# Identity multiplies on TensorE in front of waits, in a two-block transformer kernel

## The reference, cut to what matters

```python
def layer(x, xc, ...):                       # first block, twice; xc is a context of 256 tokens
    h  = modulate(x, g_norm1, sh1, sc1)      # rms norm, gain and shift
    hc = modulate(xc, g_norm1, ...)
    proj, projc = h @ w_in, hc @ w_in[:, :n_in_c]
    k, v, q = mixer_kv(...), mixer_q(...)    # low-rank latents, norms per head, rotary
    o_mla, o_gqa = blocked_attend(...), blocked_attend(...)
    o_four = fourier_mix(...)
    x = x + gt1 * merge_branches(o_mla, o_gqa, o_four, gate_cols, lp)
    x = x + gt2 * conv_ffn(modulate(x, g_norm2, sh2, sc2), lp)
    # the same for xc in layer 0 alone

def second_block(x, ...):
    for layer in range(2):                   # mixer ab: dilated attention and a gated scan
        y = _mixer_ab(x, ...) if layer == 0 else _mixer_c(x, ...)
        x = _layer_norm(DEEPNORM_ALPHA * x + y, ln_gain[layer], ln_bias[layer])
    return x
```

## Time and profile before

| | |
|---|---|
| three runs | 1990.22, 1991.87 and 1993.07 us; median 1991.87 |
| profiled execution, first to last instruction (span) | 1988.9 us; no time of its own is given beside it, the three runs lie 1.3, 3.0 and 4.2 us above |
| TensorE products, busy | 1877.4 us (94%), 12063 records |
| TensorE weight loads, busy | 1571.9 us (79%) |
| VectorE, ScalarE, GpSimd busy | 1162.5, 933.1 and 198.5 us |
| mean granted clock of TensorE | 0.983 |
| DMA | 265.36 MB, mean 133 GB/s |

### The profile page before, as it was taken

One profiled execution on the slowest core, in us unless ns is written; L12 is line 12 of the kernel. 1 busy time (PEld: TensorE's weight loads), 2 busy tenths in 40 slices (PEclk: granted clock), 3 DMA queues, 4 the chain that ended last, 5 costly groups with the idle time before them and its releaser, 6 DMA issues.

```text
span 1988.9 us, 31268 instructions
## 1 busy us (share of the span) xinstructions
PE 1877.4 (94%) x12063; PEld 1571.9 (79%) x12063; DVE 1162.5 (58%) x1802; ACT 933.1 (47%) x1427; POOL 198.5 (10%) x203
## 2 busy tenths in 40 slices
PE   5999999999998999999998889989999999899997
PEld 2875565788887888888784579989989888799996
DVE  3326566444346555523535456677744578789987
ACT  3327555323324333311436654455534656387782
POOL 4010001000011223210100000023301000100000
PEclk9999999999998999999998999989999999999999
DMA  9225668333332232232250036645557433444442
GB/s 310 91 80 169 197 221 273 97 95 95 90 110 81 89 102 94 96 116 95 85 170 6 1 88 177 191 143 181 178 190 217 158 118 104 150 151 146 146 137 101
DMA packets 262855, 265.36 MB, mean 133 GB/s; under 512 B 6342, under 2 KB 230960, under 8 KB 262752
## 3 DMA queue, kind: packets, MB, share of 16 engines
q1 hardware_dynamic: 257856, 249.32, 40.4%
q0 software_dynamic: 4448, 13.49, 2.2%
q10 hardware_dynamic: 448, 1.12, 0.2%
HBM read 262.81 MB, written 1.10 MB: 133 GB/s over the span
## 4 chain that ended last, share of the span: by engine, by line
PE 78%; DVE 12%; ACT 5%; DMA 2%; issue 2%; SPq 0%; DVEq 0%; ACTq 0%
PE bank L480 21%; PE bank L481 21%; PE bank L482 21%; PE bank L693 4%; DVE weights_fine L1839 2%; PE bank L710 2%; DMA region<-in_w_mod 2%; PE bank L538 2%; PE bank L474 2%; PE bank L527 2%; PE bank L700 1%; ACT weights_coarse L1137 1%; DVE region L2482 1%; DVE small L2164 1%; PE bank L950 0%
## 5 line engine op out<-in xcount | busy, mean ns | idle before, releaser
L1839 DVE TENSOR_TENSOR weights_fine<-region,weights_coarse 128x2048 fp32r<-128x2048 f32 (+2 forms) x181 | 417.7, 2308 | 346.8 <-ACT weights_coarse L1137 345.7
L1137 ACT CAST weights_coarse<-region 128x2048 fp32r<-128x2048 f32 (+3 forms) x185 | 355.0, 1919 | 333.0 <-PE bank L482 323.9
L480 PE MATMUL bank<-normed_coarse,weights_coarse 128*128 128x256 f32 (+1 forms) x1104 | 371.3, 336 | 9.2 <-DVE normed_fine L1977 4.3
L481 PE MATMUL bank<-normed_fine,weights_coarse 128*128 128x256 f32 (+1 forms) x1104 | 370.9, 336 | 0.0
L482 PE MATMUL bank<-normed_coarse,weights_fine 128*128 128x256 f32 (+1 forms) x1104 | 370.8, 336 | 0.0
L480 PEld LDWEIGHTS bank<-normed_coarse,weights_coarse 128*128 128x128 f32 x1104 | 212.4, 192 | 30.7 <-issue 10.1
L481 PEld LDWEIGHTS bank<-normed_fine,weights_coarse 128*128 128x128 f32 x1104 | 212.3, 192 | 20.5
L482 PEld LDWEIGHTS bank<-normed_coarse,weights_fine 128*128 128x128 f32 x1104 | 212.3, 192 | 20.4
L480 PE MATMUL bank<-x_turned_coarse,weights_coarse 128*128 128x256 f32 x616 | 177.8, 289 | 8.7 <-DVE weights_fine L1839 4.2
L481 PE MATMUL bank<-x_turned_fine,weights_coarse 128*128 128x256 f32 x616 | 175.5, 285 | 0.0
L482 PE MATMUL bank<-x_turned_coarse,weights_fine 128*128 128x256 f32 x616 | 175.5, 285 | 0.0
(11 more groups left out here) (295 smaller groups left out, 3574.4 us busy)
## 6 DMA issues: line engine op xcount, KB each, us to landing
region<-in_w_mod SPq DMA_DIRECT2D x48, 1024.0 KB, 5.3
region<-in_w_up SPq DMA_DIRECT2D x44, 1024.0 KB, 5.1
region<-in_w_in_c SPq DMA_DIRECT2D x30, 1024.0 KB, 5.2
region<-in_w_in_ab SPq DMA_DIRECT2D x20, 1024.0 KB, 5.3
region<-in_w_in SPq DMA_DIRECT2D x32, 512.0 KB, 4.7
region<-in_w_down SPq DMA_DIRECT2D x16, 1024.0 KB, 5.0
region<-in_w_in SPq DMA_DIRECT2D x14, 1024.0 KB, 5.0
region<-in_w_in SPq DMA_DIRECT2D x16, 384.0 KB, 3.5
```

The source lines that it names most:

```text
L480: nc.tensor.matmul(o, sc, mc, start=first, stop=False)
L481: nc.tensor.matmul(o, sc, mf, start=False, stop=False)
L1137: nc.scalar.copy(w_co[:, p, 0:size], raw_w[:, s, 0:size]).then_inc(coarse_ready, 1)
L1839: nc.vector.tensor_tensor(w_fi[:, p, 0:size], raw_w[:, s, 0:size], w_co[:, p, 0:size].bitcast(F32), ALU.subtract).then_inc(fine_ready, 1)
```

## The change

A helper `keep_busy(n)` is added to TensorE's stream. It multiplies the identity (`ident`, 128x128, float32) by itself n times into the first 128 columns of bank 7, each time as a new sum. It waits for nothing, signals nothing, and nobody reads the result. It is called in 16 places in the course of the program, 144 multiplies in all: before the first norm (9) and in it (4), at the last transposes of layer 0's second norm (11) and behind it (9), in layer 1's first norm (12), before the last head transposes of layer 1 (8), before both attentions (6 each), before layer 1's merge (9), before its second norm (10), in it (4) and behind it (18), and in the two `turn_x` (3 and 7; 22 and 6). No other engine's stream is changed.

```diff
--- before.py
+++ after.py
@@ -556,6 +556,11 @@
                     pe.wait_ge(bank_read[b], n)
                 transposes([first_rows[:, m * P:(m + 1) * P] for m in range(4 * pair, 4 * pair + 4)], parts_in=MOD_ROWS)
 
+            def keep_busy(n):
+
+                for _ in range(n):
+                    nc.tensor.matmul(pb[7][:, 0:P], ident[:, :], ident[:, :], start=True, stop=True)
+
             def xn_transposes(t):
                 seen_next(xn_ready)
                 for half in range(2):
@@ -577,9 +582,12 @@
             def norm(nt, project=False, started=0):
 
                 for t in range(nt):
+                    if t == nt - 1 and not project:
+                        keep_busy(11 if nt == 4 else 4)
                     if t >= started:
                         xn_transposes(t)
                     if project and t == 1:
+                        keep_busy(4 if started else 12)
                         w = split_weights(KD, COLS)
                     if project and t >= 1:
                         seen_next(h_ready)
@@ -656,6 +664,8 @@
                         following = products(*tiles[s + 1])
                     if l == 0:
                         mod_chunk()
+                    elif s + 1 == len(tiles):
+                        keep_busy(8)
                     mla_transposes(kind, t, raw[s % 2], copied)
                     gqa_transposes(kind, t)
 
@@ -868,29 +878,38 @@
             xn_transposes(0)
             first_product(7)
             first_transposes(3)
+            keep_busy(9)
 
             for l in range(DEPTH):
                 norm(4, project=True, started=int(l == 0))
                 project(l)
                 latents(l)
                 heads_prep(l)
+                keep_busy(6)
                 attend(l)
                 if l == 0:
                     mod_chunk(last=True)
                     reads = list(u.reads)
                 fourier(l, (lambda: gate_transposes(reads)) if l == 0 else None)
+                if l:
+                    keep_busy(9)
                 merge(l)
                 mix_out(l)
+                if l:
+                    keep_busy(10)
                 norm(items_of(l))
+                keep_busy(18 if l else 9)
                 ffn_up(l)
                 ffn_down(l)
 
 
-            def turn_x(updates_of):
+            def turn_x(updates_of, idle):
                 for t in range(2):
+                    keep_busy(idle[t])
                     for half in range(2):
                         pe.wait_ge(x_done, updates_of(t, half))
                         transposes([x_tok[:, t, k * P:(k + 1) * P] for k in range(4 * half, 4 * half + 4)])
+                keep_busy(idle[2])
                 evacuated()
 
             def features():
@@ -992,7 +1011,7 @@
                             w.append([v.rearrange("p (k n) -> p k n", k=WIDE_ROWS) for v in (last_co, last_fi)])
                         end(token_rows(accs[t][:, :], y2T, WIDE_ROWS * part, t, w[half], WIDE_ROWS, WIDE, False, True))
 
-            turn_x(lambda t, half: X_UPDATES - 1 + t)
+            turn_x(lambda t, half: X_UPDATES - 1 + t, (0, 3, 7))
             w = split_weights(KD, P)
             feature_product(w, KD, 0, xT, SEQ)
             for _ in range(4):
@@ -1043,7 +1062,7 @@
             seen_next(y_ready)
             out_last(rest)
 
-            turn_x(lambda t, half: X_UPDATES + 2 * t + half + 1)
+            turn_x(lambda t, half: X_UPDATES + 2 * t + half + 1, (0, 22, 6))
             for _ in range(3):
                 features()
             tokens()
```

## The result

The changed kernel took 1978.62 us (median; 1978.16 to 1979.29 in 4 runs) against 1991.9 (1990.22 to 1993.07). The ratio is 0.9925, 95% interval 0.9911 to 0.9938: faster by 0.75%, some 13.3 us where 16.9 were forecast, and inside the range of 1969 to 1984. The profiled execution has a span of 1976.8 us against 1988.9, 12.1 less.

The account below looks back on a forecast made before the run. TensorE, busy 94% of the span, was taken to bound the kernel, with nine stretches at half clock. Their gains of 17.7 us less 1 for new falls, off the 1991.9 median, gave 1975.2, said as 1975.0; range 1969 to 1984.

Parts of the forecast that it names:

- The price of a multiply: In the blocks: 0.223 us each at full clock, 0.43 at half; 144 multiplies add 32 us of TensorE work.
- The blocks fit: In the 16 places: blocks fill 80 to 95% of a hole and end before the awaited event at full clock.
- the block of 4 in the last norm: Before the transposes at 1301.13: 0.9 us in a 0.28 us hole delays them 0.6 us, but costs nothing.
- VectorE takes over: In the norms (44.6): VectorE's chain limits the gain to its idle 1.93 and 0.65 us before line 1959: 2.5 us.
- rival 2: All nine low stretches: every microsecond at half clock is worth half itself, 30.7 us of 61.5, giving 1961; chance 0.04.
- the term for falls that come anew: At two long holes left open (1052.95 and 1633.17): falls cost 1.5 us each, perhaps 3; counted as 1 us.
- The open hole before 1621: The unfilled 2.80 us hole before the products at 1633.17 in the old kernel; a fall would cost 1.5 us, perhaps 3.
- the first (some falls come anew): Any place: some falls stay or come anew, four stretches at 2 us each, gain 9, giving 1983; chance 0.14.
- The fourth: Behind the stretches: regained time is lost at once because weights and loads come no earlier, giving 1989; chance 0.06.
- The third: In the blocks: identity products don't hold the clock, run at 0.43 us each and overrun by 9.6, giving 2001.5; chance 0.06.

Follow-up runs that it names:

- the last of the kernels with more blocks: The changed kernel plus blocks of 10 in two open holes, single multiplies among the 32-row products, and blocks of 7 in four layer 0 holes: 1979.68 us.

## Why the prediction was right, and what it missed

The forecast was 1975.0 us and the chance 0.70 went to 1971 to 1979; 1978.62 lies at the upper end of that. The mechanism held, stretch by stretch. The distance in time between the same VectorE instruction in the two profiles, read before and behind each place (positive: the changed kernel is ahead), gives what each stretch brought:

| stretch before | distance, before it and behind it | measured | forecast |
|---|---|---|---|
| 44.6 | -1.78, 0.66 | 2.4 | 2.5 |
| 198.2 | 0.67, 2.34 | 1.7 | 1.8 |
| 604.4 | 2.88, 5.12 | 2.2 | 2.3 |
| 976.5 | 5.12, 7.40 | 2.3 | 2.4 |
| 1078.9 | 7.40, 10.67 | 3.3 | 2.6 |
| 1171.0 | 10.64, 12.13 | 1.5 | 1.5 |
| 1300.7 | 12.05, 13.62 | 1.6 | 1.8 |
| 1502.1 | 13.62, 14.80 | 1.2 | 1.3 |
| 1717.2 | 10.36, 12.14 | 1.8 | 1.5 |
| sum | | 17.9 | 17.7 |

**The price of a multiply** taken from the scan's products (0.223) held: 0.22 in the blocks. **The blocks fit**: the stalls left are 0 to 0.8 us (up to 0.6 were forecast), and the block of 4 in the last norm behaved as the steps said, the transposes come at once behind it (1289.54, no idle time) and VectorE's readers lose nothing by it. **VectorE takes over** in the norms: its idle time of 1.93 us is gone and the 0.65 is 0.24. That a low stretch is worth what the chain through it gives, and not half its length, was the step that separated 1975 from rival 2's 1961: 17.9 us came of 61.5.

What the prediction had too small is the term for falls that come anew, 1 us in the sum. By the same distances it measured 4.4. The open hole before 1621 cost 1.4 (11.77 to 10.36), just what the prediction had put on one such fall. The fall at 1529.0 cost 3.0 (14.80 to 11.77) and stood in no step: the prediction took idle time as the one cause of a fall, and the kernels with 32 rows showed that work on few rows does it too. The second profile of the changed kernel gives 1.5 and 3.0 us for the same two falls.

A second term, at nothing in the prediction, is the start of the program, where VectorE's distance goes to -1.78 before the first block. TensorE's timeline there, of the kernel before and then of the changed one:

```profile
35.81 1.04 PE L538 MATMUL bank<-region,sil_c 128*2 128x256 f32 x16 [1.68 <-DMA region<-in_w_mod]
36.78 1.44 PE L474 MATMUL bank<-ident,region 98*128 98x98 f32 x12
...
35.94 1.89 PE L538 MATMUL bank<-region,sil_c 128*2 128x256 f32 x16 [1.35 <-DMA region<-in_w_mod]
37.76 2.62 PE L474 MATMUL bank<-ident,region 98*128 98x98 f32 x12
```

The same sixteen passes and twelve transposes took nearly twice as long. TensorE still worked at its slow pace from the start, which the kernel before had left by 35.81; the table of stretches doesn't show this, as it gives 1.00 there. The change has no part in it, no block runs before 42.53: in the second profile of the changed kernel the same rows take 1.04 and 1.44 us, and its span is 1974.0. So 1.3 of the 1.8 us are this pace (the distance was -0.46 before), and it is an accident of the execution.

The account of the spans is then 17.9 for the stretches, less 4.4 for the new falls, less 1.8 for the start, and 0.5 more in the attention of layer 0, where waits for weight loads shrank: 12.2, against 12.1 measured. The medians differ by 13.3. The profiled run of the changed kernel took 1.8 us more than its span; with the same addition, an estimate, the profiled execution of the kernel before took 1990.7, 1.2 less than its median. So the forecast missed by the two terms above, 3.4 and 1.8 us, and was helped by small ones the other way, 1.2 of it in the base; that it came out no further off than 3.6 is in part luck. The first term is a real gap in the reasoning.

Of the rivals, the first (some falls come anew) is what took part of the gain, with two new stretches at 4.4 us together where it had four at 2 us each. The fourth has one instance, the wait for a load at 335 us in the last of the kernels with more blocks. The third is true of blocks with 32 rows and false of these. The second is refuted by 17.9 us against its 30.7.

Why the clock holds through one open hole in an execution and falls at it in another stays open. The kernel before held through 2.80 and 2.84 us and fell after 1.48; the changed kernel held through 2.84 and fell behind 2.80.

## What to carry to other kernels

Read the granted clock in short stretches, and price a stretch at half clock by the chain through it. Filling the waits in front of such stretches with idle multiplies pays when they end before the event, at a price taken from a like product of the same trace; beyond the hole they cost nearly their full length, and at half clock twice that. Let the filler use all 128 rows: 32 failed, and no number between was tried. The columns may be few, and float32 transposes do as well. Real products on few rows can bring the clock down by themselves.

## What the runs showed of the hardware that was not expected

- Products on 32 rows of the array let the clock fall from 2.4 to 1.2 GHz with TensorE 100% busy (the 7.03 us for sixteen passes against 3.72). They did so as filler and as real work, with dense numbers (1999.55 us) and with nearly all zeros (2006.33).
- Products on all rows but 32 columns hold it at 1.00 (one run, 1978.25 us, mean clock 0.996).
- Float32 transposes hold it as products do (ratio 0.9922 against 0.9925).
- Being busy did not bring the clock back: in the kernel with blocks of 32 rows it stayed at 0.50 for 17.1 us from 1305.8, with TensorE busy throughout. The block ended at 1318.8, products on all rows followed, and the clock rose at 1322.9.
- At the start of the program the pace doubled at different times in different executions: twelve transposes took 1.44 us in one profile of the changed kernel and 2.62 in the other.
